# Prompt attention with its logits made from high and low parts of keys and queries

## What is computed

```python
kv = rmsnorm(h, g_kv) @ w_kv                       # (2048, 1024) -> keys, values: 16 heads of 64
proj = rmsnorm(h, g_norm_b[i]) @ w_in_b[i]         # queries and gate
q = proj[..., :SB_WIDTH] * SB_HEAD_DIM ** -0.5
z = jnp.einsum('bqhd,bkhd->bhqk', q_blk, k) + bias[None, :, None, None]
lneg = jnp.where(valid, jax.nn.log_sigmoid(-z), 0.0)
suffix = lax.cumsum(lneg, axis=3, reverse=True) - lneg
w = jnp.where(valid, jnp.exp(jax.nn.log_sigmoid(z) + suffix), 0.0)
return jnp.einsum('bhqk,bkhd->bqhd', w, v)         # then * silu(gate) @ w_out_b
```

## Time and profile before

| | us |
|---|---|
| median of 3 runs | 3538.48 (3536.65 to 3539.49) |
| the profiled execution | 3538.79 |
| its span, from the first to the last instruction | 3537.2 |

### The profile page before, as it was taken

How to read it: one execution, slowest core, us unless ns; L and a number is a source line. 1 busy time by engine, 2 the same in 40 slices (tenths; PEclk the granted TensorE clock), 3 DMA queues, 4 the chain that set the end, 5 groups by cost and what they waited for, 6 DMA issues and landing times. The chain is left out here.

```text
span 3537.2 us, 49773 instructions
## 1 busy us (share of the span) xinstructions
PE 3277.4 (93%) x17836; PEld 2402.0 (68%) x17836; DVE 1617.4 (46%) x1930; ACT 1391.9 (39%) x2281; POOL 915.2 (26%) x917
## 2 busy tenths in 40 slices
PE   7999999678699699999999799999999999499998
PEld 6999999344388599999999344444444444366665
DVE  5111121566533321111122488888888787334442
ACT  5111111444411211111111477778778786234442
POOL 0000000455401000000000366666666565000000
PEclk9999999788899899999999699999999999799999
DMA  4222121433444422212221632232323200799995
GB/s 145 72 72 70 59 64 49 153 128 123 164 137 166 156 96 72 67 66 65 72 67 54 175 100 84 70 92 84 108 49 105 63 28 12 272 340 369 349 344 204
DMA packets 223746, 439.01 MB, mean 124 GB/s; under 512 B 22997, under 2 KB 130202, under 8 KB 211514
## 3 DMA queue, kind: packets, MB, share of 16 engines
q1 hardware_dynamic: 203626, 334.04, 28.8%
q0 software_dynamic: 19952, 102.77, 8.2%
HBM read 312.76 MB, written 124.00 MB: 123 GB/s over the span
## 5 line engine op out<-in xcount | busy, mean ns | idle before, releaser
L1656 POOL TENSOR_TENSOR att_w<-att_w,att_rest 128x1023 f32<-128x1023 f32 (+7 forms) x384 | 613.2, 1599 | 375.3 <-DVE att_rest L1621 372.2
L455 PE MATMUL projb_acc<-projb_x_hi,projb_w_hi 128*128 128x416 f32 x1280 | 452.8, 354 | 27.0 <-DVE projb_x_lo L445 27.0
L455 PE MATMUL projb_acc<-projb_x_hi,projb_w_lo 128*128 128x416 f32 x1280 | 450.8, 352 | 0.0
L455 PE MATMUL projb_acc<-projb_x_lo,projb_w_hi 128*128 128x416 f32 x1280 | 450.3, 352 | 0.0
L1528 PE MATMUL att_z<-att_k,att_q 64*128 64x512 f32 (+3 forms) x1280 | 403.4, 590 | 1.8 <-ACT att_w L1579 1.7
L1571 ACT ACTIVATE att_rest<-att_z,att_bias 128x1024 f32<-128x1024 f32 (+7 forms) x384 | 333.0, 867 | 135.6 <-PE att_z L1528 113.9
L1492 PEld LDWEIGHTS att_wT_acc<-const_ident,att_w 128*128 128x128 f32 x2176 | 232.7, 141 | 216.2 <-issue 116.1
L1621 DVE TENSOR_TENSOR_SCAN att_rest<-att_rest,att_zero 128x128 f32<-128x128 f32 (+7 forms) x256 | 358.6, 1406 | 21.9 <-ACT att_rest L1571 21.2
L292 PE MATMUL proja_acc<-proja_x_hi,proja_w_hi 128*128 128x416 f32 x1000 | 354.2, 354 | 0.8 <-DVE proja_x_lo L265 0.7
L292 PE MATMUL proja_acc<-proja_x_hi,proja_w_lo 128*128 128x416 f32 x1000 | 352.4, 352 | 0.0
L292 PE MATMUL proja_acc<-proja_x_lo,proja_w_hi 128*128 128x416 f32 x1000 | 350.3, 350 | 0.0
(11 more groups left out here) (236 smaller groups left out, 4726.7 us busy)
## 6 DMA issues: line engine op xcount, KB each, us to landing
smp_k_pages<-in_cache_k SPq DMA_DIRECT2D x128, 512.0 KB, 6.5
smp_v_pages<-in_cache_v SPq DMA_DIRECT2D x128, 512.0 KB, 6.8
proj_b<-projb_out POOLq DMA_DIRECT2D x32, 1040.0 KB, 4.7
proj_a<-proja_out POOLq DMA_DIRECT2D x24, 1040.0 KB, 4.5
att_q<-proj_b SPq DMA_DIRECT2D x64, 256.0 KB, 4.1
att_k<-proj_b SPq DMA_DIRECT2D x14, 1024.0 KB, 13.3
proja_w_raw<-in_w_in_a SPq DMA_DIRECT2D x24, 512.0 KB, 4.1
gla_vgT<-proj_a SPq DMA_DIRECT2D x24, 512.0 KB, 5.8
```

Source lines behind the costliest of these rows:

```text
L455: mm = pe.matmul(acc[:, q, 0:size], w[:, b, k, :], x[:, k, at:at + size], start=(k == 0 and w is w_hi and x is x_hi), stop=(k == KD - 1 an ...
L1656: pool.tensor_tensor(these, these, passed[:, 1:size], ALU.mult).then_inc(w_made, 1)
```

## The change

`project` gets blocks of three kinds, "parts" (keys and queries), "plain" (values) and "gate". Of a "parts" block ACT copies each span a second time, into `slab[:, 0]` as fp32r (the high part), DVE subtracts it from PSUM into `slab[:, 1]` (the low part), PE waits for that too before it writes over the span, and POOL's queue stores both parts of the prompt's 2048 columns to two new tensors in DRAM; ACT waits for these stores before the next block's first high part. The block itself is stored as before. In `prompt_attention` `k2` holds on one half of the partitions the high part of the keys and on the other the low part, alternating with each 512 keys; `q_hi` and `q_lo` hold each part twice. The logits of 512 keys are then one fp32r product of 128 rows (q_hi with high and low keys at once) and one of 64 rows (q_lo with the high keys); the products of a tile's two pieces come as wide, wide, low, low. The low x low product is left out. Raw keys and values are loaded in pieces of 512 tokens into two buffers, each asked for two turns ahead, and `k_tok` is stored after each turn instead of once for each pair.

In `project`:

```diff
+        def high(at, size):
+            return slab[:, 0, at:at + size].bitcast(F32R)
+
+        def low(at, size):
+            return slab[:, 1, at:at + size].bitcast(F32R)
...
                     act.activation(out[:, b, at:at + size], acc[:, q, 0:size],
-                                   ACT.Sigmoid if gate else ACT.Copy).then_inc(copied, 1)
+                                   ACT.Sigmoid if kind == "gate" else ACT.Copy).then_inc(copied, 1)
+                    if kind == "parts":
+                        if q == 0 and from_tile(no, 1):
+                            act.wait_ge(parts_stored, no * 32)
+                        act.activation(high(at, size), acc[:, q, 0:size], ACT.Copy).then_inc(high_made, 1)
...
+                    elif kind == "parts":
+                        dve.wait_ge(high_made, no * n_spans + (q + 1))
+                        dve.tensor_tensor(low(at, size), acc[:, q, 0:size], high(at, size).bitcast(F32),
+                                          ALU.subtract).then_inc(low_made, 1)
...
                         pe.wait_ge(copied, (n - 1) * n_spans + (q + 1))
+                    if last_kind == "parts":
+                        pe.wait_ge(low_made, last_no * n_spans + (q + 1))
...
+                if kind == "parts":
+                    pool.wait_ge(low_made, no * n_spans + n_spans)
+                    pool.dma_start(parts[0][ds(no * P, P), :], high(0, SEQ).bitcast(F32)).then_inc(parts_stored, 16)
+                    pool.dma_start(parts[1][ds(no * P, P), :], low(0, SEQ).bitcast(F32)).then_inc(parts_stored, 16)
```

In `prompt_attention`, SP:

```diff
+            def head_rows(part, at):
+                return parts[part][at:at + P, :].rearrange("(h p) n -> p h n", p=HD)
+
+            def load_k_span(pair, u, sem):
+                for half in range(2):
+                    sp.dma_start(k2[half * HD:(half + 1) * HD, pair % 2, :, u * BANK:(u + 1) * BANK],
+                                 head_rows(0 if u % 2 == half else 1, k_parts + pair * P)[:, :, u * BANK:(u + 1) * BANK]
+                                 ).then_inc(sem, 16)
+
             def load_k(pair):
...
+                for u in range(NCH):
+                    load_k_span(pair, u, in_k[pair % 2])
 
             def load_q(pair, g):
...
+                for part, dst in enumerate((q_hi, q_lo)):
+                    for half in range(2):
+                        sp.dma_start(dst[half * HD:(half + 1) * HD, g, :, :],
+                                     head_rows(part, q_parts + pair * P)[:, :, g * BANK:(g + 1) * BANK]
+                                     ).then_inc(in_q[g], 16)
...
-            load_raw(0)
+            load_raw(0, 0)
+            load_raw(0, 1)
...
+                elif kind == "turn":
+                    m, = x
+                    for e in range(2):
+                        sp.wait_ge(copied[e], ring_no[(kind, pair, m)] + 1)
+                    if m < 2:
+                        load_raw(pair, m + 2)
+                    elif pair + 1 < PAIRS:
+                        load_raw(pair + 1, m - 2)
+                    sp.dma_start(k_out.rearrange("(t p) n -> p t n", p=P)[:, 4 * m:4 * m + 4, pair * P:(pair + 1) * P],
+                                 k_tok[:, m % 2, :, :]).then_inc(k_stored[m % 2], 16)
```

PE's logits and ACT's new wait:

```diff
-                for half, at in enumerate(range(0, size, BANK)):
-                    rows, end = slice(half * HD, (half + 1) * HD), min(at + BANK, size)
-                    pe.matmul(z_ps[:, n % 2, at:end], q2[rows, t // 4, h, (t % 4) * P:(t % 4 + 1) * P],
-                              k2[rows, pair % 2, h, lo + at:lo + end], start=carried or end < size, stop=True,
-                              skip_group_check=True).then_inc(z_made, 1)
+                tile = slice((t % 4) * P, (t % 4 + 1) * P)
+                ends = [(at, min(at + BANK, size)) for at in range(0, size, BANK)]
+                for at, end in ends:
+                    pe.matmul(z_ps[:, n % 2, at:end], q_hi[:, t // 4, h, tile].bitcast(F32R),
+                              k2[:, pair % 2, h, lo + at:lo + end].bitcast(F32R),
+                              start=carried or end < size, stop=False, skip_group_check=True)
+                for half, (at, end) in enumerate(ends):
+                    rows = slice(half * HD, (half + 1) * HD)
+                    pe.matmul(z_ps[:, n % 2, at:end], q_lo[rows, t // 4, h, tile].bitcast(F32R),
+                              k2[rows, pair % 2, h, lo + at:lo + end].bitcast(F32R),
+                              start=False, stop=True, skip_group_check=True).then_inc(z_made, 1)
...
-                    if m == 0 and pair:
-                        act.wait_ge(kv_stored, 32 * pair)
-                    act.activation(k_tok[:, 4 * m:4 * m + 4, :], wT_ps[:, 0, :].rearrange("p (t n) -> p t n", n=P),
+                    if m >= 2 or pair:
+                        act.wait_ge(k_stored[m % 2], 16 * (2 * pair + m // 2))
+                    act.activation(k_tok[:, m % 2, :, :], wT_ps[:, 0, :].rearrange("p (t n) -> p t n", n=P),
```

More of the change, by code:

```diff
@@ L338, in _, with project @@
             pool.wait_ge(stored[1], 16 * (blocks // 2))
-def project(nc, c, name, xnT, jobs, first_gate):
+def project(nc, c, name, xnT, jobs, parts):
     with ExitStack() as stack:
@@ new lines, in project @@
+        n_parts = sum(count for _, _, kinds, _, _ in jobs for kind, count in kinds if kind == "parts")
+        def high(at, size):
+            return slab[:, 0, at:at + size].bitcast(F32R)
+        def low(at, size):
+            return slab[:, 1, at:at + size].bitcast(F32R)
+        def over_blocks(engine, step, skip_first=False):
+            last, done, used = (None, 0), 0, {"parts": 0, "plain": 0, "gate": 0}
+            for j, (_, _, kinds, _, _) in enumerate(jobs):
+                jb = 0
+                for kind, count in kinds:
+                    no = used[kind]
+                    if done or not skip_first:
+                        step(j, jb, done, done // 2, 0, (kind, no), last)
+                    step(j, jb + 1, done + 1, done // 2, 1, (kind, no + 1), (kind, no))
+                    with engine.Fori(1, count // 2) as i:
+                        for b in range(2):
+                            step(j, i * 2 + (jb + b), i * 2 + (done + b), i + done // 2, b, (kind, i * 2 + (no + b)),
+                                 (kind, i * 2 + (no + b - 1)))
+                    used[kind], last = no + count, (kind, no + count - 1)
+                    jb, done = jb + count, done + count
@@ L405, in _, with step @@
                 act.activation(x_hi[:, k, :], slab[:, k % 2, :], ACT.Copy).then_inc(x_hi_made, 1)
-            def step(j, jb, n, i, b, width, gate, follows_gate):
+            def step(j, jb, n, i, b, this, last):
+                kind, no = this
                 for q, (at, size) in enumerate(spans):
@@ L447, in _, with products @@
             over_blocks(dve, step, skip_first=True)
-            multiply_gate(n_blocks - 1, 1)
+            finish(n_blocks - 1, 1, "gate", 0)
         @block.tensor
         def _(pe):
-            def products(b, width, k, q):
+            def products(b, k, q):
                 at, size = spans[q]
@@ L480, in _, with step @@
         def _(pool):
-            def step(j, jb, n, i, b, width, gate, follows_gate):
-                if gate:
-                    pool.wait_ge(gate_made, (n - first_gate) * n_spans + n_spans)
+            def step(j, jb, n, i, b, this, last):
+                kind, no = this
+                if kind == "gate":
+                    pool.wait_ge(gate_made, no * n_spans + n_spans)
                 else:
```

138 lines of the change are left out of this document (56 added, 82 removed).

## The result

The changed kernel takes 3491.8 us (median of 4 runs, 3490.1 to 3492.2) where the kernel before took 3538.5 (median of 3; a fourth run of it took 3788.7 us in a slower state and is left out): a ratio of 0.9868 [0.9848, 0.9887], 47 us less. Some 13 us of the forecast gain did not come. The profiled execution took 3490.1 us, its span is 3488.2, 49.0 shorter than before.

The account below looks back on a forecast made before the run. PE was taken to bound the kernel, with DVE close behind in the attention and binding "rest". From 3538.8 us, 64 off for eight pairs, plus 1 for the projection and 3 for the attention's start, gave 3479 us, range 3452 to 3528.

Parts of the forecast that it names:

- C at 128 only: Rival, attention: only split products of 128 columns run at four passes, costing 1.9 us per pair; 3494 us, chance 0.12.
- +1: Projection: only the first block, whose five spans end together, shows the extra copies, subtractions and stores; 1 us more.
- 0.06 + (N/2400 + 0.014) + 0.09 + (N/2400 + 0.20): Attention, PE: us for a masked one-piece tile of width N after the change: mask, wide product, layout change, low product.
- the tenth that the forecast had taken off: Attention, per head pair: 8.9 us of gain cut to 8.0 for three engines waiting on each other.
- I keep half, 0.8: Attention phase "below": of PE's 1.5 us saving per pair 0.8 stays, as DVE needs 24.02 us and shares a buffer.
- +3 between -3 and +12: Attention start: later first keys and late raw pieces, less logits savings at half clock; 3 us more in all.
- ACT shows idle time on stores: Sign that the forecast is wrong: ACT idle on stores in projection or attention; it expected ACT never late.
- B: Rival, attention: the two low products do not overlap, so only 2.0 us per pair is gained; 3527 us, chance 0.08.
- C: Rival, attention: split products of 128, 256 and 384 columns run at four passes; 4.9 us more per pair, 3582, chance 0.05.
- D: Rival, attention: each wide product shows its weight load, 80 per pair at 0.12 us; 3529 us, chance 0.03.
- A: Rival, attention: DVE, ACT and PE interlock and half of the gain is lost to waits; 3511 us, chance 0.15.
- E: Rival, attention: nothing moves (3543 us), or PE falls to half clock in "first" (3600 us); chance 0.05.

Follow-up runs that it names:

- hybrid: Changed kernel with the low product on all 128 rows in tiles of one piece only; ratio 0.9825 to the kernel before.
- mask_later: Changed kernel with the mask product behind the wide products of its tile instead of ahead of them; ratio 0.9867 to the kernel before.
- v_on_act: Changed kernel with ACT instead of DVE copying the turned values in the two turns in "below"; ratio 0.9858 to the kernel before.
- no_low: Changed kernel with the products of q_lo and the high keys left out; 3427 us, ratio 0.9697 to the kernel before.
- after_again: The changed kernel itself, unedited, run once more beside later runs; ratio 0.9882 to the kernel before.
- spread_full: Changed kernel with all low products on 128 rows, mask behind wide products outside "first", three early attention loads spread over pair 0; ratio 0.9778 to the kernel before.
- full_low: Changed kernel with every low product on all 128 rows, low x low included; ratio 0.9811 to the kernel before.
- late_loads: Changed kernel with three loads (4 MB) moved from ahead of the attention's loop to behind pair 0's fourth turn; ratio 0.9883 to the kernel before.

## Why the prediction was right, and where it was off

The sign, the stage and the bound of each phase were right, and 3491.8 lies in the forecast's own range, near its upper end. By the time alone the rival "C at 128 only" (3494) is nearer than the forecast (3479); it takes the steps below to tell them apart. The forecast promised 13 us too much. On the profiled executions it promised 60 and 49.0 came. The 11 are 8 + 3 + 3 in the pairs (1 to 6, the last, the first), less 2 ahead of the first scan (the forecast had put +1 there, -1.2 came) and 1 behind the last. The 2 and the 1 are luck: ahead of the first scan the change costs 5 us, and 6 came from stages that it does not touch.

**The price of a wide product (most of the 8 us).** This is the term that was mis-sized. Of the cost of a masked tile, 0.06 + (N/2400 + 0.014) + 0.09 + (N/2400 + 0.20), two terms held at 256 keys: the low product took 0.310 where 0.307 was said, and the change of layout 0.09 (0.29 with it, 0.20 without, by `hybrid`). The mask took 0.03 where 0.06 was said, and the wide product 0.20 where 0.121 was said. The 0.014 came from the average of three products and half a set of transposes in the earlier trace rows. The row of the first of the three, which those rows leave out, shows the error already; it starts 0.31 us ahead of the second (3101.14), and the other two take 0.24 and 0.23:

```profile
3100.83 0.48 PE L1989 MATMUL smp_y_acc<-smp_w_hi,smp_oT_hi 128*128 128x512 f32 x1
```

There, as in a carried beat, the 0.09 of the first product is made up by transposes that end 0.08 earlier, so the sum of the group came out right and so did the carried beat (2.93, said: 2.90). A mask between them breaks that. Over the four widths the tiles took 0.523, 0.634, 0.752 and 0.876 us where 0.471, 0.577, 0.684 and 0.791 were said: 1.05 too little for the 16 tiles of "first", which kept 2.87 instead of 4.0. In tiles of two pieces the same error is 0.06 to 0.08, between 0.5 and 0.6 for eight: "middle" kept 1.69 instead of 2.1 and "above" 1.43 instead of 1.8. Over pairs 1 to 6 the shortfall of these three phases is 11.5 us, that of "below" 2.8, and "rest" gave 0.8 too much; from the 13.5 goes the tenth that the forecast had taken off without a row behind it, 0.9 a pair or 5.4, and 8 are left (6.67 a pair instead of 8.0). So that tenth hid part of the error: without it the forecast would have been 3472. What makes these 0.09 us was not tried. The weight loads differ, in the groups from 2230 to 2820 us (busy us, mean ns, idle before):

```profile
L1565 PEld LDWEIGHTS att_z<-att_k,att_q_hi 128*128 128x128 f32 x394 | 62.7, 192 | 1.3
...
L1560 PEld LDWEIGHTS att_z<-const_diag_mask,const_ident_bf 128*128 128x128 bf16 x154 | 15.0, 97 | 32.0 <-issue 32.0
```

A load of 0.19 us behind a mask that takes 0.03 would fit, but a wide product behind values, which take 1.0 us, costs as much over its columns (0.12 at 256, `mask_later`), so this is argued, not shown.

**"Below" (2.8 of the same 8).** "I keep half, 0.8" was a guess at an interlock, and 0.34 came. The reading that DVE binds there was right (`v_on_act`). What was not seen is what DVE's order does: two gate products and two copies of turned values are queued behind scans of 2.34 us, and PE waits for them (2.6 us without work in the phase). "Rest" gained 0.33 for 0.2: right, and `no_low` shows that 0.2 more is all there is.

**The last pair (3 us).** The forecast multiplied one steady pair by eight; pair 7 gained 4.7. Of the 3.3 missing, 1.3 are the steady pair's own shortfall and 1.5 lie in its "middle", 23.29 us in this execution and 21.79 in `after_again`. The two stretches, the changed kernel first:

```profile
2869.98:2893.27 23.29, 23.29 (x134) 13.23 (x130) 20.03 (x18) 17.90 (x23) 14.23 (x9) 0.93 0.08 24
...
2869.93:2891.72 21.79, 21.79 (x134) 12.45 (x130) 20.03 (x18) 17.88 (x23) 14.21 (x9) 1.00 0.08 25
```

The work is the same and the granted clock is not: it is 0.50 for 3.4 us from 2871.2, 1.4 us after PE has waited 1.52 us for the gate product on DVE. In `after_again` PE waits 1.51 us at the same place and the clock stays at 1.00.

**The start (3 us in pair 0, and more ahead of it).** Said: +3 between -3 and +12, so pair 0 at -5; measured -2.1, with "first" at +4.25. Of the named parts, the first keys came 2.5 us later after the first load (said: 1.5) and the second group 1.6 (said: 1.5). The mechanism was the named one: raw pieces 2 and 3 come late, with 9.3 us waited where 0 to 8 was said, and PE ran at the half clock (0.50) in most of this "first", as it did before; what that gave back was not measured by itself. What the prediction missed is that the price inside pair 0 is not one of the bytes but of their order: in `spread_full` pair 0 takes 118.7 us, 1.8 more than a steady pair of that kernel.

**The projection.** +1 was said, for the first block; PE's products took 0.6 less, and 2.6 came in a place that no term covered, GpSimd's drain at the end of the stage. The sum behind the blocks holds (parts land in 6.0 and 8.9 us, the next block's part of ACT has room). Its test was stated too strictly, though: "ACT shows idle time on stores" is true of this trace, for 91 us, and means nothing, since PE does not wait for ACT there.

**The rivals.** B is out: the two low products start 3 to 4 ns apart. C is out: behind a mask a split product of 128 columns takes 0.14 us and one of 256 0.20 (`hybrid`), and one of 128 behind a wide one 0.12 (`full_low`), so one pass each. The sign that was named, 0.12 at most, fails by 0.02 behind a mask for the reason above. D is out: the second wide product's step is 0.231 us in `full_low` with a weight load of its own onto the same rows. By this step the rule of the Trainium skill (TensorE: Matmul & The Clock Gate, Part 3, The mechanism), that a load overlaps products only when the row group differs, does not describe this stream. The wide-to-wide step was named as 0.23 and is 0.318, again the first product's extra 0.09. A is right in kind and about 3 us in size, all in "below". E's clock did not come in any phase of pairs 1 to 6 (1.00 throughout). It did fall for 3.4 us each in pair 0's "below" (behind a wait of 1.78 us; the phase took 24.48 us, 23.20 in `after_again`) and in pair 7's "middle", and more often in `no_low`.

## What to carry to other kernels

A product on half of the array's rows is cheap only in pairs: where one stands alone between products of 128 rows, fill the other half, even with terms that nobody needs. Take the price of a new instruction from a row with the same neighbour on either side, since a group's sum hides which member pays for the change. Before a difference ahead of the changed stretch is called a cost or a gain, measure the stages that the change leaves alone, and the border between two stages by itself. When a crowd of loads is moved, look at what is issued right behind it in its new place, and when an engine with slack is queued in order between two that have none, count what stands behind its longest instruction.

## What was new about the hardware

- A change from 128 to 64 rows costs 0.09 us at the full clock, and the way back 0.10 to 0.25, at widths from 256 to 512 columns.
- At 256 columns a first fp32r product behind a mask takes 0.09 us over its columns, a following one ahead of transposes 0.01; behind fp32 transposes nearly all of it comes off the transposes' step (0.85 to a wide product, 0.93 to a mask).
- SyncE stood for 10.9 us at an issue behind 16 loads of 256 KB and a store of 1 MB issued within 12.3 us; most issues before that took 0.6 each (`late_loads`).
- GpSimd's drain at the end of a projection took 2.10 us after 25 stores of 1 MB or less on its queue, 2.67 after 32 and 5.28 after 64, and all engines wait for it. What sets its length was not tried.
- In "below", behind a wait of 1.87 us, PE ran at 1.2 GHz for 6.8 us in three pairs, and behind one of 1.86 us in three others at the full clock (`no_low`). In the changed kernel it ran at 1.2 GHz for 3.4 us behind a wait of 1.52 us, and in `after_again` at the full clock behind one of 1.51 us.
